# A two-layer float32 trunk on one core: seven products for the first mixer's values, paired half-height rate products, and router tiles moved by ScalarE

## The chip, the cores and the metric

One core of one Trainium2 chip runs the whole program, in float32. The metric is the device time of one execution in microseconds (us); of the kernel before, three runs stand here and their median counts. Lower is better. The engines are TensorE (PE in the rows, with its weight loads as PEld), VectorE (DVE), ScalarE (ACT), GpSimd (POOL) and SyncE (SP), which issues most DMAs. Each runs its own instructions strictly in order, and they wait for each other by semaphores.

## The reference

The input is 512 tokens of width 1024 and 256 memory tokens. There are two layers; layer 0 mixes tokens by RWKV-7, layer 1 by stick-breaking attention. Each mixer is followed by a cross-attention into the memory and by a mixture of experts (top 1 of 4 groups, then top 2 of 8 experts in it, 32 experts in all).

```python
def _rwkv7_time_mix(h, mix, wr, wk, wv, w0, w1, w2, a0, a1, a2, ...):
    xr, xw, xk, xv, xa, xg = [h + dx * mix[i] for i in range(N_MIX)]
    r = xr @ wr;  k = xk @ wk;  v = xv @ wv                  # 512x1024 by 1024x1024
    w_log = -softplus(-(w0 + tanh(xw @ w1) @ w2)) - 0.5      # rates: 64 inputs, 1024 outputs
    a = sigmoid(a0 + (xa @ a1) @ a2)                         # rates: 64 inputs, 1024 outputs
    kk = (k * k_k).reshape(B, S, H, N)
    kk = kk / maximum(norm(kk, axis=-1, keepdims=True), 1e-12)
    ...                                                      # state recurrence over heads
def _hierarchical_moe(h, wg, bg, we, be, w1, w3, w2):
    g_logits = t @ wg + bg;  e_logits = t @ we + be          # router: 4 + 32 columns
    ...                                                      # top-1 group, top-2 experts, SwiGLU
```

## The kernel before

The program has stages that follow each other on TensorE: the six projections of the first mixer, the "pair stage" (the recurrence for eight pairs of heads), the group norm, the memory's keys and values, the output product `rwo`, then for each layer cross-attention (`xq`, attention, `xo`), routing, and the experts.

**Large products.** A 1024x1024 weight arrives as two units of 2 MB in a ring of three. `project_T` (L568 to L573) takes eight output chunks of eight products each, 128x512 elements a product. Most other weights use Strassen-like "seven products": both operands are cut in quarters, VectorE forms eight sums of quarters (`sum_of`, L646, counted by the semaphore `quarters`), and TensorE takes 14 groups (`seven_T_pe`, L731 to L776: 8 products of 128x256 a group; `seven_pe`, L577: 4 products of 128x512 a group). Groups 4 to 7 wait for sum 5, groups 8 and 9 for sum 7, and groups 10 to 13 for sum 8. Eight of the groups are copied out by ScalarE (`T_out`, L779), the other six added onto them by VectorE (`add_T`, L786; `add_group`, L659). A group's bank is reused only when its last content has been copied or added.

**First mixer around the change.** TensorE's order is w1, a1, g1 (L891), wr and wk (seven products), then the rates (`rates_pe`, L935 and L936: for each of eight chunks one product with w2 and one with a2, both over 128 inputs, where half of each weight is zero), then two chunks of wv (L572), eight norm sums (`norms_pe`, L945), and six chunks of wv. ScalarE turns each chunk of rates into two sigmoids (L953, L955); TensorE's chunk j waits for the sigmoids of chunk j-2. Then ScalarE squares the keys (L959), copies two chunks of wv out, takes one square root over all norms (L912), makes the first pair's exponentials (L1052 to L1072), and copies out the rest of wv (L832). VectorE, after wk's last adds (L786): a scan and a difference (L1014, L1017) once all sigmoids are there, eight `max` operations on the norm sums (L970), then for each of eight chunks a reciprocal (L973) and a product (L975), and last five "factors" of pair 0 (L1024 to L1045), without which the pair stage (L1275) can't begin. TensorE's first pair product also waits for GpSimd's copy (L1110).

**Router around the change.** Group 8 to 13 of `xo` (L615) complete the rows of the hidden state h in order of tiles of 128 tokens: tile 0 is complete with group 8, tile 1 with 10, tile 2 with 11, tile 3 with 13 (`TILE_DONE`), each after VectorE's add (L659). Between these groups, at places that a table gives as (group, k), TensorE turns eight blocks of a tile (`late_turn`, L511), and later takes the router's logits of that tile (`route_logits`, L2025) and the ranks (`route_ranks`, L2042, L2043). Turned blocks lie in three banks, so block n waits until block n-3 has been moved out. Even blocks are moved by ScalarE (L521), odd ones by VectorE (L523); of tile 3 ScalarE moves all. VectorE runs the choice of experts as a chain of some 20 small operations a tile (`group_and_first`, L2133 to L2143, and `second`, L2148 to L2157), and `place` (L2162 to L2167). ScalarE squares and sums each tile (L2083, L2093), takes the root (L2087), scales the rows (L2073) and issues their store (L2075).

```python
    for n in range(4): mix(n, *MIXES[n])
    left_sums(vec, "wr", RK_S1)
    sums_T(vec, "wr", xm[1], RK_S1, RK_TS["wr"], R_)
    ...
    add_group(vec, xo, 8, 0, 1)
    evac(0)
    add_group(vec, xo, 9, 1, 1, 0, over=6)
    scale(0); group_and_first(0)
    add_group(vec, xo, 10, 1, 0, over=9)
    second(0)
    evac(1)
    add_group(vec, xo, 11, 2, 1)
```

## Time and profile before

| what | value |
|---|---|
| runs, us | 1753.58, 1757.02, 1759.72; median 1757.02 |
| profiled execution | 1754.93 us, span 1753.1 us |
| TensorE's granted clock, mean | 0.953 |
| busy share of the span: PE, DVE, ACT, POOL | 89%, 48%, 24%, 9% |
| chain that ended last: PE, issue, DVE, ACT | 70%, 7%, 5%, 4% |
| DMA | 312.89 MB, mean 178 GB/s |

A float32 product is two MATMUL instructions in the trace, so 64 products read as "x128". Timeline rows give start, time on the engine, engine, line, operation, operands and count; what stands in brackets is the idle time just before and what ended it. "PEclk" in the rows by stretch is TensorE's granted clock as a share of full speed: 1.00 is 2.4 GHz, 0.50 is 1.2 GHz.

### The profile page before, as it was taken

The page shows a single profiled execution, that of the slowest core. Times are in us where ns is not written, and L with a number is a line of the kernel's source. Part 1 is how long each engine was busy: PE and PEld are TensorE (multiplying, and loading weights), DVE is VectorE, ACT ScalarE, POOL GpSimd, SP SyncE. Part 2 cuts the span into 40 slices and gives each one's busy share as a digit, 9 for nine tenths or more (in the row PEclk, how much of TensorE's full clock was granted, in tenths as well). Part 3 has the DMA queues.
Part 4 walks back from the last instruction along what each step waited for, and adds up shares of the span by engine and source line. Part 5 has one row for each costly group of instructions (what it writes and reads, how often), then busy time and mean ns, then how long its engine had stood idle before and what let it go on. Part 6 is the DMA issues. An engine that isn't in the chain of part 4 may idle for free.

```text
span 1753.1 us, 28204 instructions
## 1 busy us (share of the span) xinstructions
PE 1568.8 (89%) x12141; PEld 953.5 (54%) x12141; DVE 833.0 (48%) x1416; ACT 421.3 (24%) x833; POOL 165.1 (9%) x185
## 2 busy tenths in 40 slices
PE   4999989998799999879877899999999996988785
PEld 2786468887474685444323368745558544333332
DVE  5651766664384625444222174447643554431225
ACT  2103245554300212211000130117421312100002
POOL 2000132330000000011111100000000001111101
PEclk8999999999799999969998999999999996999898
DMA  7026200000532521259999952220024124999994
GB/s 241 1 96 240 90 3 4 4 4 4 216 116 76 214 74 52 101 225 412 423 424 423 371 199 96 96 95 2 1 109 180 25 87 171 391 423 425 425 413 185
DMA packets 81503, 312.89 MB, mean 178 GB/s; under 512 B 17776, under 2 KB 18856, under 8 KB 56608
## 3 DMA queue, kind: packets, MB, share of 16 engines
q1 hardware_dynamic: 69280, 282.76, 41.1%
q0 software_dynamic: 10944, 24.10, 3.7%
q10 hardware_dynamic: 1152, 4.19, 0.6%
q8 instruction: 97, 1.59, 0.4%
q14 instruction: 30, 0.25, 0.0%
HBM read 305.81 MB, written 33.29 MB: 193 GB/s over the span
## 4 chain that ended last, share of the span: by engine, by line
PE 70%; issue 7%; DVE 5%; ACT 4%; DMA 1%; POOL 1%; PEld 0%; DVEq 0%; POOLq 0%; ACTq 0%
PE PS L2482 14%; PE PS L615 13%; PE PS L748 10%; PE PS L1275 7%; PE PS L2507 6%; PE PS L1609 2%; PE PS L572 2%; PE PS L2467 2%; PE PS L586 2%; PE PS L1585 1%; PE PS L1857 1%; PE PS L1878 1%; PE PS L511 1%; PE PS L1868 1%; PE PS L2025 1%
## 5 line engine op out<-in xcount | busy, mean ns | idle before, releaser
L748 PE MATMUL PS<-arena,ring 128*128 128x256 f32 x1152 | 251.2, 379 | 0.0
L748 PEld LDWEIGHTS PS<-arena,ring 128*128 128x128 f32 x1152 | 218.4, 190 | 31.2 <-issue 1.4
L615 PE MATMUL PS<-ring,arena 128*128 128x512 f32 x400 | 177.8, 596 | 0.7 <-ACT arena L1823 0.7
L2482 PE MATMUL PS<-ring,arena 128*64 128x512 f32 x512 | 127.8, 657 | 43.6 <-issue 40.5
L2482 PE MATMUL PS<-arena 128*64 128x512 f32 x512 | 125.7, 647 | 21.1 <-issue 18.3
L2490 DVE TENSOR_TENSOR arena<-PS,arena 128x256 f32<-128x256 f32 x32 | 13.6, 424 | 252.5 <-PE PS L2497 232.4
L615 PEld LDWEIGHTS PS<-ring,arena 128*128 128x128 f32 x400 | 75.5, 192 | 89.0 <-issue 88.0
L2482 PEld LDWEIGHTS PS<-ring,arena 128*64 128x64 f32 x512 | 43.0, 151 | 126.5 <-issue 122.8
L2487 ACT ACTIVATE arena<-PS 128x256 f32<-128x256 f32 x32 | 12.3, 384 | 359.1 <-PE PS L2482 359.1
L2482 PEld LDWEIGHTS PS<-arena 128*64 128x64 f32 x512 | 42.8, 148 | 102.4 <-issue 98.9
L572 PE MATMUL PS<-arena,ring 128*128 128x512 f32 (+1 forms) x256 | 84.5, 492 | 0.0
L786 DVE TENSOR_TENSOR arena<-arena,PS 128x512 f32<-128x512 f32 x48 | 31.5, 684 | 106.8 <-PE PS L748 106.8
L1275 PE MATMUL PS<-ring 64*64 64x64 f32 (+1 forms) x3072 | 75.4, 239 | 5.3 <-ACT ring L1124 3.1
L659 DVE TENSOR_TENSOR h<-h,PS 128x512 f32<-128x512 f32 x64 | 43.2, 685 | 76.9 <-PE PS L615 76.8
L779 ACT ACTIVATE arena<-PS 128x512 f32<-128x512 f32 x48 | 28.3, 596 | 211.8 <-PE PS L748 211.8
L1275 PEld LDWEIGHTS PS<-ring 64*64 64x64 f32 x3072 | 70.9, 137 | 13.6 <-issue 5.3
L1124 ACT ACTIVATE ring<-PS 128x512 f32<-128x512 f32 (+1 forms) x88 | 63.0, 753 | 50.8 <-PE PS L1275 48.4
L615 PE MATMUL PS<-arena 128*128 128x512 f32 x160 | 74.7, 612 | 0.0
L2382 POOL MEMSET arena<- 128x1024 f32 x4 | 3.8, 969 | 721.3 <-PE PS L615 721.3
L646 DVE TENSOR_TENSOR arena<-arena 128x1024 f32<-128x1024 f32 x40 | 49.0, 1224 | 47.6 <-PE PS L748 41.3
L572 PEld LDWEIGHTS PS<-arena,ring 128*128 128x128 f32 x256 | 49.7, 195 | 34.3 <-issue 30.6
L521 ACT ACTIVATE arena<-PS,gainT 128x128 f32<-128x128 f32 x88 | 27.7, 364 | 134.5 <-PE PS L511 134.3
(326 smaller groups left out, 2413.4 us busy)
## 6 DMA issues: line engine op xcount, KB each, us to landing
arena<-in_moe_w SPq DMA_DIRECT2D x96, 1024.0 KB, 16.2
ring<-in_moe_w SPq DMA_DIRECT2D x96, 1024.0 KB, 14.7
ring<-in_sb_wqkv SPq DMA_DIRECT2D x6, 2048.0 KB, 9.2
ring<-in_xa_wkv SPq DMA_DIRECT2D x4, 2048.0 KB, 15.6
ring<-in_xa_wq SPq DMA_DIRECT2D x4, 2048.0 KB, 8.7
ring<-in_xa_wo SPq DMA_DIRECT2D x4, 2048.0 KB, 14.5
h<-in_x SPq DMA_DIRECT2D x8, 512.0 KB, 5.0
ring<-in_rw_wr SPq DMA_DIRECT2D x2, 2048.0 KB, 14.4
```

What stands on the lines that cost most here:

```text
L572: ins = pe.matmul(PS[:, BANK_OF[g], 0:n], ring[:, u % RING, k, P * (j % 4):P * (j % 4) + P], xt[:, k, 0:n], start=(k == 0), stop=(k == KC ...
L586: ins = pe.matmul(PS[:, BANK_OF[g], :], xt[:, k, P * t:P * t + P], ring[:, (u0 + half) % RING, k, :], start=(k == 0), stop=(k == KC - 1))
L615: ins = pe.matmul(PS[:, BANK_OF[g], :], rows(k), cols[:, k, :], start=(k == 0 and not grows), stop=(k == 3), skip_group_check=grows)
L646: vec.tensor_tensor(out, a, b, op).then_inc(S("quarters"), 1)
L659: ins = vec.tensor_tensor(v, v, group_out(vec, g), ALU.add)
L748: ins = pe.matmul(PS[:, BANK_OF[g], M * c:M * c + M], rows[:, k, o:o + P], cols[:, k, :], start=(c + k == 0 and not grows), stop=(k == 3), ...
L1124: act.activation(dst, src, ACT.Copy).then_inc(S("pair_act_out"), 1)
L1275: return pe.matmul(out, lhs, rhs, start=start, stop=True, skip_group_check=True)
L1609: ins = pe.matmul(PS[:, BANK_OF[g], :], memV[:, m, XD * x + P * v:XD * x + P * v + P], probT[x % 2][:, m, :], start=(m == 0), stop=(m == 1))
L2467: ins = pe.transpose(bank(k // 4, 4, P)[:, k % 4, 0:rows], xg[p][0:rows, k::KC], ident[0:rows, 0:rows])
L2482: ins = pe.matmul(bank(2, 2, F)[r, :, :], xgT[p][:, k, r], w[a][:, :, k, :], start=(k == 0), stop=(k == KC - 1))
L2507: ins = pe.matmul(PS[r, 6 + half, :], hidT[:, k, r], w2e[p][a][:, k, 512 * half:512 * half + 512], start=(k == 0), stop=(k == 1))
```

## The change

It does three things. (1) wv gets 14 groups and eight sums like wr and wk; its sums and adds are put into VectorE's order around the norms, with the eighth sum and the last adds behind the loop of reciprocals. (2) The two rate products of a chunk take only the 64 inputs that are not zero, one on the lower and one on the upper half of the rows; GpSimd no longer clears the other halves. (3) In both routers tile 0 is still shared, but tiles 1 and 2 are moved by ScalarE alone, as tile 3 was; ScalarE squares a tile before it moves the blocks (tile 3 after); and TensorE turns a tile in four quarters of two blocks, one behind each k of a group. GpSimd's clearing of GT moves behind wv.

```diff
-    ("wr", 14, "AAVVAAAAAVVAVV"), ("wk", 14, "AAVVAAAAAVVAVV"), ("wv", 8, "A"),
+    ("wr", 14, "AAVVAAAAAVVAVV"), ("wk", 14, "AAVVAAAAAVVAVV"), ("wv", 14, "AAVVAAAAAVVAVV"),
...
-            pool.memset(w2s[HD:P, :], 0.0).then_inc(S("rates_padded"), 1)
-            pool.memset(a2s[0:HD, :], 0.0).then_inc(S("rates_padded"), 1)
...
+        def late_on_act(n):
+            return n % 2 == 0 or (LATE[n // (NT * KC)][:3] == "ffn" and n % (NT * KC) >= KC)
...
-        def late_turn(pe, name, t, ready):
+        def late_turn(pe, name, t, ready, ks=range(KC)):
             ready(pe, t)
-            for k in range(KC):
+            for k in ks:
...
+        WV_S1, WV_TS = at(28, [4, 512]), in_place(xm[1], at(30, [4, M]))
...
                     rates_pe(pe)
-                    project_T(pe, g, UNITS.index(name), x_, T, ready, range(2))
-                    norms_pe(pe)
-                    project_T(pe, g, UNITS.index(name), x_, T, ready, range(2, 8))
+                    seven_T_pe(pe, name, x_, WV_S1, WV_TS, ready, {(3, 1): lambda: norms_pe(pe)})
...
-            evac_T(act, FIRST["wv"], V_, chunks=range(2))
+            T_out(act, "wv", V_, range(2))
...
-            evac_T(act, FIRST["wv"], V_, chunks=range(2, 8))
+            T_out(act, "wv", V_, range(2, 8))
...
-                pe.matmul(PS[:, 4 + 2 * (j % 2), :], w2s[:, P * j:P * j + P], twa, start=True, stop=True)
-                pe.matmul(PS[:, 5 + 2 * (j % 2), :], a2s[:, P * j:P * j + P], twa, start=True, stop=True)\
+                pe.matmul(PS[:, 4 + 2 * (j % 2), :], w2s[half(0), P * j:P * j + P], twa[half(0), :], start=True, stop=True)
+                pe.matmul(PS[:, 5 + 2 * (j % 2), :], a2s[half(1), P * j:P * j + P], twa[half(1), :], start=True, stop=True)\
...
             vec.wait_ge(S("notfirst_ready"), 2)
+            left_sums(vec, "wv", WV_S1)
             vec.wait_ge(S("pre_sig"), 2 * KC)
             sums(vec, 0)
+            sums_T(vec, "wv", xm[1], WV_S1, WV_TS, V_)
             for j in range(KC):
                 vec.wait_ge(S("pre_summed"), j + 1)
                 vec.tensor_scalar(KK[:, j, :], PS[:, 4 + j % 4, :], 1e-24, None, ALU.max).then_inc(S("pre_norm"), 1)
...
                                          in1=KK[:, j, :], op0=ALU.mult, op1=ALU.mult).then_inc(S("kk_ready"), 1)
+            last_sum(vec, "wv", xm[1], WV_TS)
+            last_adds(vec, "wv", V_)
...
-            pool.wait_ge(S("proj_filled"), FIRST["wv"] + 8)
+            pool.wait_ge(S("proj_filled"), FIRST["wv"] + 14)
+            pool.memset(GT, 0.0).then_inc(S("zeros_ready"), 1)
...
-                     {(9, 1): lambda: late_turn(pe, ffn, 0, ready), (10, 1): lambda: route_logits(pe, l, 0),
-                      (11, 1): lambda: late_turn(pe, ffn, 1, ready), (12, 1): lambda: route_logits(pe, l, 1),
-                      (12, 2): lambda: late_turn(pe, ffn, 2, ready), (12, 3): lambda: route_ranks(pe, l, 0),
+                     {**turns(9, 0), **turns(11, 1), **turns(12, 2), (10, 1): lambda: route_logits(pe, l, 0),
...
                 ready(act, t)
-                late_evac(act, name, t, xTE, 0, 1 if last else 2)
+                if last:
+                    late_evac(act, name, t, xTE, 0, 1)
                 act.activation(tnE[:, t, 0:end], h[:, t, 0:end], ACT.Square, accum_out=total)
+                if not last:
+                    late_evac(act, name, t, xTE, 0, 1 if t else 2)
...
-            evac(1)
             add_group(vec, xo, 11, 2, 1)
             scale(1)
             group_and_first(1)
             second(1)
-            evac(2)
             place(0)
```

In `turns(12, 2)` the logits of tile 1 come behind the second quarter and the ranks of tile 0 behind the fourth.

The order of instructions shows where each piece lands. The first place is VectorE at the end of the first mixer's projections, in the changed kernel; L966 and L968 are the reciprocals and their products (L973 and L975 before), L638 is a sum of quarters, L779 an add of a group, L1019 to L1040 the five factors, L1188 the first operation of the pair stage.

```order
L966 RECIPROCAL arena<-arena 128x512
L968 SCALAR_TENSOR_TENSOR arena<-arena,prm 128x512
L638 TENSOR_TENSOR arena<-arena 128x1024
L779 TENSOR_TENSOR arena<-arena,PS 128x2x256 x6
L1019 TENSOR_TENSOR arena<-h 128x512
L1021 TENSOR_TENSOR arena<-h 128x512
L1026 SCALAR_TENSOR_TENSOR arena<-arena,prm,h 128x512
L1033 SCALAR_TENSOR_TENSOR arena<-arena,h 128x512
L1040 TENSOR_TENSOR arena<-arena,h 128x512
L1188 TENSOR_TENSOR ring<-PS,masks 128x8x64
```

Before, the factors came right behind the last reciprocal and product; now the eighth sum and six adds stand between.

The second place is TensorE in `xo`, groups 11 to 13 of layer 0, before the change: L615 are the products of `xo`, L511 the turns, L2025 the logits, L2042 and L2043 the ranks.

```order
L615 MATMUL PS<-ring,arena 128x512 x2
L511 MATMUL PS<-ident,h 128x128 x8
L615 MATMUL PS<-ring,arena 128x512 x4
L2025 MATMUL PS<-arena 128x36 x8
L615 MATMUL PS<-ring,arena 128x512
L511 MATMUL PS<-ident,h 128x128 x8
L615 MATMUL PS<-ring,arena 128x512
L2042 MATMUL PS<-arena,masks 128x32
L2043 MATMUL PS<-arena,ones 128x32
```

And the same place in the changed kernel, from group 12 on, with its own line numbers:

```order
L607 MATMUL PS<-ring,arena 128x512
L503 MATMUL PS<-ident,h 128x128 x2
L607 MATMUL PS<-ring,arena 128x512
L503 MATMUL PS<-ident,h 128x128 x2
L2029 MATMUL PS<-arena 128x36 x8
L607 MATMUL PS<-ring,arena 128x512
L503 MATMUL PS<-ident,h 128x128 x2
L607 MATMUL PS<-ring,arena 128x512
L503 MATMUL PS<-ident,h 128x128 x2
L2046 MATMUL PS<-arena,masks 128x32
L2047 MATMUL PS<-arena,ones 128x32
```

The turns of tile 2 have moved from one place to four, and two of its quarters now stand ahead of the logits of tile 1.

The third place is ScalarE in the same stretch in the changed kernel: L2088 squares a tile, L513 moves blocks, L2094 is the root, L2077 scales rows and L2079 stores them.

```order
L2088 ACTIVATE arena,sumsq<-h 128x1024
L513 ACTIVATE arena<-PS,gainT 128x128 x8
L2094 ACTIVATE rms<-sumsq,ffn_eps 128x1
L2077 ACTIVATE arena<-h,rstd 128x1024
L2079 DMA normed_rows<-arena 128x1024
L2088 ACTIVATE arena,sumsq<-h 128x1024
L513 ACTIVATE arena<-PS,gainT 128x128 x8
```

Tile 2's square, and behind it the moves of tile 2's blocks, come after the scaling and the store of tile 0's rows, as they did; but there are eight moves a tile now in place of four, and the square stands ahead of them.

## Rows read from the trace of the kernel before

**Rows 1.** The chain of waits: start, us, what.

```profile
199.89 27.44 issue
...
763.53 3.56 DMA arena<-normed_rows,table
```

**Rows 2.** Timeline of the first mixer's rates and of the values' first chunks.

```profile
151.59 1.02 PE L935 MATMUL PS<-arena 128*128 128x512 f32 x2
...
155.23 0.69 ACT L953 ACTIVATE arena<-PS,prm 128x512 f32<-128x512 f32 x1 [0.37 <-PE PS L936]
...
155.81 0.68 ACT L955 ACTIVATE arena<-PS,prm 128x512 f32<-128x512 f32 x1
...
165.32 13.90 PE L572 MATMUL PS<-arena,ring 128*128 128x512 f32 x32
...
166.90 1.22 DVE L1014 TENSOR_TENSOR_SCAN h<-h,arena 128x512 f32<-128x512 f32 x1 [13.67 <-ACT arena L955]
...
179.06 7.03 PE L945 MATMUL PS<-arena,hones 128*128 128x512 f32 x16
```

**Rows 3.** Timeline from the last norm to the first pair product.

```profile
185.93 41.36 PE L572 MATMUL PS<-arena,ring 128*128 128x512 f32 x96
...
186.85 3.62 ACT L912 ACTIVATE arena<-arena 128x4096 f32<-128x4096 f32 x1 [5.69 <-DVE arena L970]
...
190.50 3.35 DVE L973 RECIPROCAL arena<-arena 128x512 f32<-128x512 f32 x1 [3.68 <-ACT arena L912]
...
222.31 0.75 DVE L975 SCALAR_TENSOR_TENSOR arena<-arena,prm 128x512 f32<-128x512 f32 x1
...
225.44 0.68 DVE L1045 TENSOR_TENSOR arena<-arena,h 128x512 f32<-128x512 f32 x1
...
228.22 1.68 PE L1275 MATMUL PS<-arena 64*64 64x128 f32 x80 [0.94 <-POOL arena L1110]
```

**Rows 4.** Timeline, TensorE in wr and wk: products of 128x256.

```profile
82.53 41.60 PE L748 MATMUL PS<-arena,ring 128*128 128x256 f32 x192
```

**Rows 5.** Timeline, VectorE's sums for wk.

```profile
110.77 2.29 DVE L646 TENSOR_TENSOR ring<-arena,ring 128x2048 f32<-128x2048 f32 x1
113.09 2.48 DVE L646 TENSOR_TENSOR arena<-arena 128x1024 f32<-128x1024 f32 x2
```

**Rows 6.** By stretch: busy us of PE, PEld, DVE, ACT, POOL, then PEclk, DMA.

```profile
33.00:38.00 5.00, 4.71 (x6) 1.44 (x7) 5.00 (x9) 0.00 (x0) 0.00 (x0) 0.50 0.52 191
738.00:740.00 2.00, 2.00 (x6) 1.19 (x5) 0.69 (x3) 1.62 (x4) 0.00 (x0) 0.50 0.24 41
```

**Rows 7.** Timeline of layer 0's router up to the last tile.

```profile
722.13 0.69 DVE L659 TENSOR_TENSOR h<-h,PS 128x512 f32<-128x512 f32 x1
...
725.96 1.05 ACT L2083 ACTIVATE arena<-h 128x1024 f32<-128x1024 f32 x1
...
727.34 1.14 ACT L2073 ACTIVATE arena<-h,rstd 128x1024 f32<-128x1024 f32 x1
...
729.51 1.87 PE L2025 MATMUL PS<-arena 128*128 128x36 f32 x16
...
735.81 0.60 DVE L523 TENSOR_SCALAR arena<-PS,gainT 128x128 f32<-128x128 f32 x2
...
736.21 0.63 PE L511 MATMUL PS<-ident,h 128*128 128x128 f32 x3 [2.89 <-DVE arena L523]
...
739.24 0.22 DVE L2162 TENSOR_TENSOR arena<-arena,PS 128x64 f32<-128x64 f32 x1 [1.43 <-PE PS L2043]
...
743.94 0.26 DVE L2133 SCALAR_TENSOR_TENSOR arena<-PS,rstd,arena 128x36 f32<-128x36 f32 x1 [1.38 <-PE PS L2025]
...
747.46 0.60 PE L511 MATMUL PS<-ident,h 128*128 128x128 f32 x3 [1.46 <-DVE h L659]
```

**Rows 8.** Timeline of layer 1's router: end of tile 1's logits, turn of tile 3.

```profile
1443.42 1.10 PE L615 MATMUL PS<-ring,arena 128*128 128x512 f32 x2
...
1460.66 0.60 PE L511 MATMUL PS<-ident,h 128*128 128x128 f32 x3 [1.46 <-DVE h L659]
```

More of the change, by code:

```diff
@@ L775, in chunks, with T_out @@
             return dst[:, 2 * i:2 * i + 2, M * half:M * half + M]
-        def T_out(act, name, dst):
-            for n, i, half in ((0, 0, 0), (1, 1, 0), (4, 2, 0), (5, 3, 0), (6, 2, 1), (7, 3, 1), (8, 0, 1), (11, 1, 1)):
+        def T_out(act, name, dst, which=range(8)):
+            copied = (0, 0, 0), (1, 1, 0), (4, 2, 0), (5, 3, 0), (6, 2, 1), (7, 3, 1), (8, 0, 1), (11, 1, 1)
+            for n, i, half in copied[which.start:which.stop]:
                 act.activation(chunks(dst, i, half), group_out(act, FIRST[name] + n).rearrange("p (c n) -> p c n", c=2),
@@ L2176, in moe_choice_vec @@
             add_group(vec, xo, 8, 0, 1)
-            evac(0)
+            late_evac(vec, f"ffn{l}", 0, xTE, 1)
             add_group(vec, xo, 9, 1, 1, 0, over=6)
```

31 lines of the change are left out of this document (14 added, 17 removed).

## Prediction

> **What bounds the kernel now.** I read the page first: TensorE is busy 89% of the span, no other engine above half, and the chain of waits is TensorE's for 70%. So a change pays or costs only where it lets TensorE's sequence, or the engine TensorE waits for, run on sooner or later. Then I read the timeline of the two stages that the change touches. The chain's largest piece of 27.4 us in the first mixer is named "issue" [rows 1]: TensorE runs the values' chunks back to back, waiting for nothing. Beside it VectorE is hardly less loaded: from 190.50 to 222.98 it runs eight reciprocals with their products, 4.06 us each, and its last factor ends at 226.1, only 2.1 us ahead of the first pair product at 228.2 [rows 3]. The reader should see that VectorE has almost no slack there. In the router it is the reverse: TensorE waits, 2.9 us at 736.2 alone, for a block that VectorE moves late, behind its own chain of small operations [rows 7].
>
> **Part 1, the rates.** Sixteen products of 0.86 us (two instructions of 0.43) go from 151.59 to 165.32 [rows 2]. On two halves of the array they could overlap. The trace shows no products of 64 inputs by 128 outputs; the nearest row is 80 instructions on quarters of the array, 64 to 128 columns each, which end within 1.68 us [rows 3]; one by one they would need 6.0 us by their columns (32 of 128 and 48 of 64, at 0.43 us for 512), so the parts do run together. I take full overlap; nothing gained (0 us) is the other end. A chunk then takes 1.29 us from its first instruction to its last, but ScalarE needs 1.17 us for its two sigmoids (0.58 apart, [rows 2]) and chunk j waits for those of chunk j-2, so two chunks take 1.29 + 1.17 + two hand-overs of about 0.13, 2.7 us. The values' products start at 162.0 in place of 165.3, and the sigmoids end 3.3 us earlier too, at 163.5. The Trainium skill's page "TensorEngine Tiling (Array Packing)", under "Theoretical Speedup", gives up to twice the speed for 64 inputs, and under "PSUM Bottleneck" says that the emptying of PSUM may then become the limit. By the table alone the values would start at 158.5, and the sum below would be 3.5 us lower; by the second sentence, which the sigmoids' rows bear out, it stays.
>
> **Part 2, the values, up to the norms.** 64 products of 128x512 become 112 of 128x256. At 192 instructions in 41.6 us one takes 0.217 us [rows 4], so a group (16 instructions) takes 3.47 us and all 14 take 48.5, against 128 of 0.431 us, 55.1 [rows 3]: 6.6 us less work for TensorE. In return VectorE gets eight sums and ten adds. Two sums of 2.3 us [rows 5] fit into its idle 13.7 us before the scan [rows 2]: they cost nothing while that wait lasts and would cost 4.6 us without it. They need both units of the weights where the old chunks began with one; the second is asked for when wk's group 11 is done, ahead of everything else in SyncE's queue, and I take it to be there in time. Groups 0 to 3 take 13.9 us, as the two old chunks did, and end at 175.9. Behind the scan come sums of 1.2, 2.3, 1.2 and 1.2 us [rows 5] and two adds (0.7 us, as L1045 in [rows 3]), the second of which needs group 3, so it ends at 176.8, and sum 7 (2.3 us) at 179.0. Only then do the `max` operations begin. The fifth norm product needs the first of them, at 179.7, and four products of 0.86 us bring the last norm to 183.2, where it was 185.93 [rows 2, 3]: 2.7 us earlier.
>
> **Part 3, the eighth sum.** This decides. In the changed order, sum 8 stands behind the last reciprocal product, and groups 10 to 13 wait for it. From the last norm, VectorE and ScalarE need 4.6 us to the first reciprocal (one `max`, one root of 3.6 us), then 32.5 us for the reciprocals [rows 3], then 1.2 us for the sum: sum 8 is there at 221.5. TensorE has groups 4 to 9 to run meanwhile, 20.8 us plus about 2.5 us in which group 6 waits for ScalarE to leave the exponentials, and is done at 206.5. It idles for 15 us. Groups 10 to 13 take 13.9 us more. After such a gap the clock falls: when the work began at 33.3 after idle time, it was granted 0.50 until 38 [rows 6], which cost half of 4.8 us, so I add 2.4 (0 to 3). That is 237.8. Then comes what was hidden before: the last add (0.3 until it starts, 0.7) and the five factors, 3.1 us [rows 3], behind it in VectorE's order. The first pair product starts at 242.0 against 228.2: 13.8 us late. GpSimd's clearing and copy (about 1.6 us) fit beside the factors. A second gap of 4 us now stands ahead of the pair stage; after the 2.9 us gap at 736.2 the clock was 0.50 from 738 to 740 [rows 6, 7], so I add 1.5 us for small products at 1.2 GHz (0, if it holds, to 6, if the stage runs its first iteration so). First mixer: **+15.3 us** (+11 to +21). The removed clearing of two halves by GpSimd is worth nothing: TensorE's first work doesn't wait for it.
>
> The same tiling page says under "Key Properties" that a change of tiling mode drains TensorE. That would add a few tenths of a microsecond at each end of the rates, and no term of mine holds it.
>
> **Part 4, the routers.** For layer 0, TensorE's logits of tile 1 end at 731.2 (729.51 and sixteen instructions) and its turn of tile 3 begins at 747.46 [rows 7], 16.2 us later. Of these VectorE spends 4.6 us on the choice for tile 1 (to 735.8), then moves tile 2's blocks, for TensorE is stuck on them, and only at 739.24 places tile 0. From there to the turn it needs 8.2 us, of which it waits 1.4 us for logits [rows 7]. With the moves gone and the logits earlier, both waits go: 4.6 + 6.8 = 11.4 us from the logits of tile 1 to the turn of tile 3, 4.8 us less. Late next is ScalarE. Tile 1's turn can start at about 722.5 (add at 722.13 less a little). ScalarE then squares (1.05 and a read-out of 0.2, [rows 7]), moves eight blocks as TensorE turns them over group 11, takes the root at about 727.1, scales and stores tile 0's rows (from 727.34 it took 1.5 us, [rows 7]), and squares tile 2 to about 730.1. The first block of tile 2 is moved at 730.5, TensorE's third turn there waits for it some 2 us, and tile 1's logits, behind that quarter, end at 732.4, 1.1 us later than before. Net 3.6 us for layer 0. In layer 1 the same stretch is 17.2 us long (1443.42 to 1460.66, [rows 8]), 1.0 us more, so 4.6 us. What follows is kept: the gather of rows (763.53, [rows 1]) waits for the table, and the later weights' loads wait for the gather, so the whole experts' stage moves with it. Routers: **-8.2 us** (-3, if ScalarE is later still, to -13).
>
> **The sum.** +15.3 - 8.2 = +7.1 us on the profiled execution of 1754.9, which is 1762.0. The profiled execution lies 2.1 us under the median of the three runs, 1757.0; on the median the sum is 1764.1, and I give 1764.
>
> **The rivals.**
> *Forecast, 0.60:* TensorE idles some 15 us before group 10; slower by 5.3 us or more. 0.3%, 5.3 us, is about what a measurement of this kernel tells from no change.
> *The gap is there but cheap, 0.27:* the clock costs little (mixer +11.3, without the 2.4 and the 1.5) and the routers give their 8.2 or somewhat more. +3 to -1 us, 1756 to 1760: no change to be measured. For it: the clock stays at 1.00 through shorter waits. Against it: the granted 0.50 after the gap at 736.
> *The values no longer bound, 0.08, on the other side:* if groups 10 to 13 could follow group 9, TensorE would end the values at 183.2 + 34.7 = 217.9, the last add and the factors would end at 222, the mixer would gain 6.2 us, and with the routers the kernel would take 1742 to 1745. It decides by whether sum 8 is there before 204; the order speaks against it, for VectorE runs no instruction out of turn, and eight reciprocals of 3.35 us have no room to shrink. A weaker form is that the routers give 8 us or more each (every wait in 35 us gone, at most 9.5 each) against +11: 1749 to 1752.
> *No overlap of the halves, 0.05 as a case of its own, slower:* the rates take their 13.7 us, all of part 2 comes 3.3 us later, and with a cold start of the pair stage the time is 1770 to 1775.
> All cases together give faster 0.08, same 0.27, slower 0.65. The range reaches from the cheap gap to the cold pair stage, 1755 to 1773.
>
> **What would show it.** Right: in the changed trace a wait of TensorE before group 10 of wv of about 15 us, released by VectorE's sum (a 128x1024 TENSOR_TENSOR behind the last product of the reciprocals); a granted clock of 0.50 in the first 5 us after it; the first pair product near 242; rates at a step of 1.3 to 1.4 us; no wait of TensorE on VectorE's moves in the turns of tiles 1 and 2, and one of about 2 us on ScalarE's there; the turn of tile 3 some 4 us earlier against the start of `xo`. Wrong: a first pair product before 230, or a distance from the start of `xo` to the gather that hasn't shrunk.

## Result and profile after

The changed kernel took 1766.66 us (median of 7 runs, 1757.69 to 1774.28), the kernel before, run beside it, 1756.74 us: a ratio of 1.0051, 95% interval 1.003 to 1.0071. Timed again later in 12 runs it took 1763.96 us against 1756.90, a ratio of 1.0044 (1.0027 to 1.0062). So it is slower, by 8 or 9 us. The profiled execution is the fastest of its seven runs, 1757.69 us with a span of 1755.9; the span of the one before was 1753.1. So stretches of the traces are compared here, not their totals. The two profiles are also shifted against each other: the first rate product starts at 150.39 us in the changed kernel and at 151.59 in the one before. So distances from there are compared here, and not moments.

The page of the changed kernel, parts 1 and 5 (busy time, share of the span, instructions; then group, busy time and mean ns, idle time just before it and its releaser):

```profile
PE 1553.6 (88%) x12237; PEld 965.2 (55%) x12237; DVE 849.1 (48%) x1416; ACT 424.4 (24%) x849; POOL 162.7 (9%) x183
...
L740 PE MATMUL PS<-arena,ring 128*128 128x256 f32 x1344 | 295.5, 381 | 14.9 <-DVE arena L638 14.9
```

TensorE has less work than before and waits 14.9 us in one place: L740 are the products of quarters, L638 VectorE's sums. Before, the values' products waited for nothing [rows 1].

**The rates.** Timeline of the changed kernel, TensorE and ScalarE (start, time, engine, line, operation, count, idle time before), answering to [rows 2]. "64*128" is the part of the array used, 64 rows by 128 columns:

```profile
150.39 0.69 PE L926 MATMUL PS<-arena 64*128 64x512 f32 x1
...
150.93 0.59 PE L926 MATMUL PS<-arena 64*128 64x512 f32 x1
...
154.12 0.69 PE L926 MATMUL PS<-arena 64*128 64x512 f32 x1
154.15 0.69 ACT L944 ACTIVATE arena<-PS,prm 128x512 f32<-128x512 f32 x1
...
156.62 0.69 PE L926 MATMUL PS<-arena 64*128 64x512 f32 x1
...
160.17 14.08 PE L740 MATMUL PS<-arena,ring 128*128 128x256 f32 x64
```

L926 is the first product of a chunk; its partner on the other half stands in L927. The rates now take from 150.39 to 160.17, 9.8 us, where they took 13.7. Two chunks come every 2.50 us (154.12 to 156.62): TensorE's first product of the next pair of chunks waits until ScalarE has ended its sigmoids (L944, L946), which start every 0.58 us and fill 2.3 of the 2.50.

**The norms and the reciprocals.** The same timeline, VectorE, ScalarE and TensorE, answering to [rows 3]:

```profile
152.18 2.29 DVE L638 TENSOR_TENSOR arena<-ring 128x2048 f32<-128x2048 f32 x1 [0.24 <-DMA ring<-in_rw_wv]
...
178.00 3.67 PE L936 MATMUL PS<-arena,hones 128*128 128x512 f32 x8 [0.31 <-DVE arena L963]
...
186.08 3.35 DVE L966 RECIPROCAL arena<-arena 128x512 f32<-128x512 f32 x1 [3.68 <-ACT arena L904]
...
190.90 7.17 PE L740 MATMUL PS<-arena 128*128 128x256 f32 x32 [2.32 <-ACT arena L772]
...
217.89 0.75 DVE L968 SCALAR_TENSOR_TENSOR arena<-arena,prm 128x512 f32<-128x512 f32 x1
218.56 1.22 DVE L638 TENSOR_TENSOR arena<-arena 128x1024 f32<-128x1024 f32 x1
219.83 16.07 PE L740 MATMUL PS<-arena,ring 128*128 128x256 f32 x64 [14.86 <-DVE arena L638]
...
236.01 0.69 DVE L779 TENSOR_TENSOR arena<-arena,PS 128x512 f32<-128x512 f32 x1 [2.14 <-PE PS L740]
...
239.50 0.68 DVE L1040 TENSOR_TENSOR arena<-arena,h 128x512 f32<-128x512 f32 x1
240.32 2.44 PE L1270 MATMUL PS<-arena 64*64 64x128 f32 x80 [4.42 <-DVE arena L1040]
```

The reader should follow VectorE (DVE): the last reciprocal's product at 217.89, then the eighth sum at 218.56, and TensorE's group 10 starts when that sum ends, 14.86 us after group 9. Behind group 13 the last add and five factors are no longer hidden: TensorE waits another 4.42 us. From the first rate product to the first pair product are 89.9 us (240.32 less 150.39), where there were 76.6 (228.22 less 151.59).

The clock in the same stretch of the changed kernel (stretch, its length, then busy time and count of PE, PEld, DVE, ACT and POOL, granted clock, DMA share, GB/s):

```profile
210.00:220.00 10.00, 0.17 (x1) 0.17 (x2) 9.93 (x7) 0.00 (x0) 0.00 (x0) 0.51 0.00 0
...
220.00:222.00 2.00, 2.00 (x5) 1.64 (x6) 0.97 (x2) 0.00 (x0) 0.00 (x0) 0.50 0.00 0
222.00:224.00 2.00, 2.00 (x6) 1.55 (x6) 0.00 (x0) 0.00 (x0) 0.00 (x0) 0.53 0.00 0
224.00:226.00 2.00, 2.00 (x11) 1.77 (x10) 0.35 (x1) 0.00 (x0) 0.00 (x0) 1.00 0.00 0
...
240.00:242.00 2.00, 1.68 (x64) 1.71 (x68) 0.18 (x1) 0.00 (x0) 0.00 (x0) 0.74 0.00 0
242.00:244.00 2.00, 1.37 (x40) 1.18 (x37) 1.94 (x4) 0.00 (x0) 0.00 (x0) 0.50 0.03 8
```

TensorE comes back from the long wait at half speed and is at full speed again from about 224. Groups 10 to 13 take 16.07 us, 2.0 more than the 14.08 of groups 0 to 3, which are as many instructions at full speed.

**The router of layer 0**, the changed kernel's timeline, TensorE and ScalarE, answering to [rows 7] (L503 turns, L2029 logits, L607 products of `xo`; L2077 scales rows, L2088 squares, L513 moves blocks):

```profile
736.19 1.14 ACT L2077 ACTIVATE arena<-h,rstd 128x1024 f32<-128x1024 f32 x1
...
737.34 0.27 PE L503 MATMUL PS<-ident,h 128*128 128x128 f32 x1
...
737.76 1.06 ACT L2088 ACTIVATE arena<-h 128x1024 f32<-128x1024 f32 x1 [0.43 <-ACT arena L2077]
...
738.81 1.18 ACT L513 ACTIVATE arena<-PS,gainT 128x128 f32<-128x128 f32 x4
...
739.21 0.38 PE L503 MATMUL PS<-ident,h 128*128 128x128 f32 x1 [1.60 <-ACT arena L513]
739.43 1.87 PE L2029 MATMUL PS<-arena 128*128 128x36 f32 x16
...
752.82 2.66 PE L503 MATMUL PS<-ident,h 128*128 128x128 f32 x8 [2.68 <-DVE h L651]
```

VectorE's 2.89 us wait is gone. A wait of 1.60 us for ScalarE has come: the fourth block of tile 2 needs a bank that ScalarE empties only after it has scaled tile 0's rows and squared tile 2, and tile 1's logits stand behind that block. The router still comes out ahead: from the start of `xo` to the gather of layer 0 it is 689.1 to 768.99 us, 79.9, where it was 679.7 to 763.53, 83.8; in layer 1 80.7 where it was 84.7. By the traces, then, the first mixer loses 13.3 us and the routers give back 3.9 and 4.0, +5.4 in all. That lies at the lower end of what was measured: the two intervals of the ratio are +5.3 to +12.5 and +4.7 to +10.9 us.

### The profile page after: what moved, and what is told of

The parts are those of the page before. It is cut to its first block, busy times and chain, and to the rows that moved or that the text cites. A ratio compares the mean times of both kernels' runs of the same rounds, so it can differ in the third digit from the quotient of the medians.

```text
span 1755.9 us, 28430 instructions
## 1 busy us (share of the span) xinstructions
PE 1553.6 (88%) x12237; PEld 965.2 (55%) x12237; DVE 849.1 (48%) x1416; ACT 424.4 (24%) x849; POOL 162.7 (9%) x183
## 4 chain that ended last, share of the span: by engine, by line
PE 81%; DVE 7%; issue 6%; ACT 4%; DMA 1%; SPq 1%; PEld 0%; DVEq 0%; ACTq 0%; POOLq 0%
PE PS L740 18%; PE PS L2484 14%; PE PS L607 12%; PE PS L1270 7%; PE PS L2509 7%; PE PS L1605 2%; PE PS L2469 2%; PE PS L2433 2%; PE PS L564 2%; PE PS L578 2%; DVE arena L966 1%; PE PS L1581 1%; PE PS L1861 1%; PE PS L885 1%; PE PS L1882 1%
## 5 line engine op out<-in xcount | busy, mean ns | idle before, releaser
L740 PE MATMUL PS<-arena,ring 128*128 128x256 f32 x1344 | 295.5, 381 | 14.9 <-DVE arena L638 14.9
L740 PEld LDWEIGHTS PS<-arena,ring 128*128 128x128 f32 x1344 | 256.1, 191 | 53.1 <-DVE arena L638 15.7
L2484 PE MATMUL PS<-ring,arena 128*64 128x512 f32 x512 | 133.6, 681 | 54.1 <-issue 51.0
L607 PE MATMUL PS<-ring,arena 128*128 128x512 f32 x400 | 180.5, 598 | 0.7 <-ACT arena L1827 0.7
L2484 PE MATMUL PS<-arena 128*64 128x512 f32 x512 | 117.2, 611 | 14.3 <-issue 11.6
L607 PEld LDWEIGHTS PS<-ring,arena 128*128 128x128 f32 x400 | 74.8, 193 | 83.3 <-issue 82.3
L779 DVE TENSOR_TENSOR arena<-arena,PS 128x512 f32<-128x512 f32 x56 | 36.8, 684 | 121.3 <-PE PS L740 121.3
L772 ACT ACTIVATE arena<-PS 128x512 f32<-128x512 f32 x56 | 32.9, 595 | 248.1 <-PE PS L740 248.1
L638 DVE TENSOR_TENSOR arena<-arena 128x1024 f32<-128x1024 f32 x44 | 54.9, 1249 | 47.7 <-PE PS L740 41.3
L607 PE MATMUL PS<-arena 128*128 128x512 f32 x160 | 72.3, 595 | 0.0
L2509 PE MATMUL PS<-ring,arena 128*64 128x512 f32 x256 | 58.5, 598 | 1.0 <-issue 1.0
L1851 DVE TENSOR_TENSOR_SCAN arena<-arena 128x128 f32<-128x128 f32 (+3 forms) x64 | 48.3, 809 | 22.9 <-ACT arena L1813 22.9
L2509 PE MATMUL PS<-arena 128*64 128x512 f32 x256 | 58.5, 598 | 1.0 <-issue 1.0
## 6 DMA issues: line engine op xcount, KB each, us to landing
ring<-in_xa_wo SPq DMA_DIRECT2D x4, 2048.0 KB, 13.8
ring<-in_rw_wr SPq DMA_DIRECT2D x2, 2048.0 KB, 13.3
```

What stands on the lines that cost most here:

```text
L607: ins = pe.matmul(PS[:, BANK_OF[g], :], rows(k), cols[:, k, :], start=(k == 0 and not grows), stop=(k == 3), skip_group_check=grows)
L638: vec.tensor_tensor(out, a, b, op).then_inc(S("quarters"), 1)
L740: ins = pe.matmul(PS[:, BANK_OF[g], M * c:M * c + M], rows[:, k, o:o + P], cols[:, k, :], start=(c + k == 0 and not grows), stop=(k == 3), ...
L779: ins = vec.tensor_tensor(v, v, group_out(vec, FIRST[name] + n).rearrange("p (c n) -> p c n", c=2), ALU.add)
L1851: vec.tensor_tensor_scan(att[m][a][:, 0:nn][:, ::-1], fail[m][a][:, T - nn:T][:, ::-1], from_query[:, T - nn:T][:, ::-1], 1.0, ALU.mult, A ...
L2484: ins = pe.matmul(bank(2, 2, F)[r, :, :], xgT[p][:, k, r], w[a][:, :, k, :], start=(k == 0), stop=(k == KC - 1))
```

## Experiments

Each was timed in five rounds beside the kernel before, whose median lay between 1754.8 and 1757.0 us. Ratios are to that kernel; 0.001 is 1.76 us, and the 95% intervals reach 0.002 to 0.003 to either side.

### Each part alone

**Rates alone** (kernel before with this):

```diff
-                pe.matmul(PS[:, 4 + 2 * (j % 2), :], w2s[:, P * j:P * j + P], twa, start=True, stop=True)
+                pe.matmul(PS[:, 4 + 2 * (j % 2), :], w2s[half(0), P * j:P * j + P], twa[half(0), :], start=True, stop=True)
...
-            pool.memset(w2s[HD:P, :], 0.0).then_inc(S("rates_padded"), 1)
```

> The kernel before with the rate products alone on 64 inputs, one on each half of the rows. My theory: in the changed kernel the eight chunks took 9.8 us from the first rate product to the first product of the values, against 13.7 before, because the halves overlap and ScalarE's two sigmoids a chunk set the step (1.25 us). Everything behind moves with it, VectorE's reciprocals too, so the first pair product comes 3.9 us sooner after the first rate product (72.7 us in place of 76.6) and the time is about 4 us lower, 0.2%. Rival: VectorE and ScalarE set the end of the values' stage in any case, so nothing is left of it at the first pair product (76.6 us).

Measured 1753.22 us against 1756.21, ratio 0.9986 (0.9965 to 1.0006). The sign isn't settled by the times. The trace of this kernel settles the mechanism: rates from 152.55 to 162.33, first pair product at 225.33, so 72.8 us between the first rate product and the first pair product, where the kernel before needs 76.6. The 3.9 us that the rates' stage is shorter (9.8 for 13.7) arrive at the first pair product but for 0.1, since the values' chunks hide nothing in front of them.

**Routers alone** (the changed kernel's `late_on_act`, quarter turns, order on ScalarE and VectorE, in the kernel before):

```diff
-                      (11, 1): lambda: late_turn(pe, ffn, 1, ready), (12, 1): lambda: route_logits(pe, l, 1),
...
+                     {**turns(9, 0), **turns(11, 1), **turns(12, 2), (10, 1): lambda: route_logits(pe, l, 0),
...
-            evac(1)
...
-            evac(2)
```

> The kernel before with the two routers' part alone. Theory: the whole is a sum of independent stages, and this one gives 3.9 us in layer 0 and 4.0 us in layer 1 (the shortening from the start of xo to the gather that the changed kernel's trace shows), so about 8 us less, 0.45%. Rival: part of what the routers gave in the changed kernel's trace was luck of the clock, and it gives under 4 us in all.

Measured 1747.76 us, ratio 0.9949 (0.9928 to 0.9969): about 9 us gained.

**Values alone** (the changed kernel's PLAN, sums and adds for wv, the rates on the whole array):

```diff
-    ("wv", 8, "A"),
+    ("wv", 14, "AAVVAAAAAVVAVV"),
...
+            last_sum(vec, "wv", xm[1], WV_TS)
+            last_adds(vec, "wv", V_)
```

> The kernel before with the values' seven products alone (rates and routers as before). Theory: the distance from the first rate product to the first pair product grows from 76.6 to about 94 us (89.9 in the changed kernel, plus the 3.9 that the rates gave there), so the time is 14 to 17 us higher, 0.8 to 1.0%. Rival: the rates' gain is swallowed in the changed kernel by the wait for the eighth sum, so without it the distance is no longer than there, 90 us, and the time 10 to 13 us higher.

Measured 1777.24 us, ratio 1.0117 (1.0088 to 1.0146): about 20.5 us lost. From the timeline of this kernel, TensorE:

```profile
223.76 15.78 PE L748 MATMUL PS<-arena,ring 128*128 128x256 f32 x64 [14.86 <-DVE arena L646]
243.96 2.69 PE L1279 MATMUL PS<-arena 64*64 64x128 f32 x80 [4.42 <-DVE arena L1049]
```

The wait is 14.86 us here too. From the first rate product (150.5) to the first pair product are 93.5 us, 16.9 more than before, as expected; the median lost some 4 us beyond that, but the interval, 15.5 to 25.6 us, takes the 16.9 in. By the ratios the parts add up to -2.5 - 9.0 + 20.5 = +9.0 us, and the whole change measured +9.0 and +7.7. Each part is known to 4 or 5 us only, so that the sum hits so well is partly luck; that the loss is in the values and the routers make back a good part of it is clear.

### The eighth sum among the reciprocals

The changed kernel, with work only reordered on VectorE:

```diff
                                          in1=KK[:, j, :], op0=ALU.mult, op1=ALU.mult).then_inc(S("kk_ready"), 1)
+                if j == 3:
+                    last_sum(vec, "wv", xm[1], WV_TS)
+                if j == 4:
+                    group_evacuated(vec, FIRST["wv"] + 4)
+                    add_T(vec, "wv", 9, V_, 2, 1, 0, over=6)
+                if j == 6:
+                    add_T(vec, "wv", 10, V_, 2, 0, over=9)
-            last_sum(vec, "wv", xm[1], WV_TS)
-            last_adds(vec, "wv", V_)
+            group_evacuated(vec, FIRST["wv"] + 5)
+            add_T(vec, "wv", 12, V_, 3, 1, 0, over=7)
+            add_T(vec, "wv", 13, V_, 3, 0, over=12)
```

> The changed kernel with the eighth sum of the values moved between the fourth and the fifth reciprocal, the add of group 9 behind the fifth and that of group 10 behind the seventh; nothing is taken away. Theory: the loss is TensorE's 14.9 us wait for that sum. It then has the sum at 203.5, before it ends group 9, groups 10 to 13 follow without a gap and at full clock and end near 218.5, and VectorE's reciprocals, adds and factors end near 227: first pair product 76 to 77 us after the first rate product in place of 89.9, time 12 to 15 us under the changed kernel, 4 to 8 us under the kernel before. Rival: VectorE's total work sets the end (sums, adds and reciprocals, whatever their order), so the first pair product moves by 3 us at most, and the time stays above that of the kernel before.

Measured 1751.5 us (12 runs, 1742.39 to 1756.87), ratio 0.9959 (0.9939 to 0.9978), some 15 us under the changed kernel. Timeline of this kernel, VectorE and TensorE:

```profile
203.48 1.22 DVE L638 TENSOR_TENSOR arena<-arena 128x1024 f32<-128x1024 f32 x1
...
221.94 0.75 DVE L968 SCALAR_TENSOR_TENSOR arena<-arena,prm 128x512 f32<-128x512 f32 x1
222.61 2.00 DVE L779 TENSOR_TENSOR arena<-arena,PS 128x512 f32<-128x512 f32 x3
...
199.02 17.43 PE L740 MATMUL PS<-arena,ring 128*128 128x256 f32 x80
218.69 3.72 PE L740 MATMUL PS<-arena,ring 128*128 128x256 f32 x16 [2.24 <-DVE arena L779]
227.82 2.90 PE L1278 MATMUL PS<-arena 64*64 64x128 f32 x80 [5.41 <-DVE arena L1048]
```

Group 10 now follows group 9 without a wait (80 instructions in one row), and the distance from the first rate to the first pair product falls from 89.9 to 76.3 us. With the same work in another order the wait and the loss both go, so the 14.86 us wait is shown to be the cause. The last three rows show something more: TensorE is done with the values at 222.4 and waits 5.41 us for VectorE. The seven products save TensorE work that VectorE, busy without a break from 187.2 to 227.7, doesn't let it use: the distance is 76.3 us though the overlapped rates, which took 3.85 us off it by themselves, are in it.

### Is the idle time dear because of the clock?

Two kernels fill TensorE's idle time with products whose results nothing reads. In the changed kernel:

```diff
+            if name == "wv":
+                pe.wait_ge(S("pre_norm"), KC)
+                for n in range(15):
+                    pe.matmul(PS[:, 4, :], hones[:, :], left(name, 0, 0)[:, n % 4, :], start=True, stop=True)
             summed_quarters(pe, name, after[2])
             group(10, 0, left(name, 1, 1), t4)
...
+            for n in range(14):
+                pe.matmul(PS[:, 4, 0:P], hones[:, :], hones[:, :], start=True, stop=True)
             pe.wait_ge(S("zeros_ready"), 3)
```

> The changed kernel with work added and none removed: 15 products of 128x512 that nothing reads fill TensorE's idle 14.86 us between group 9 and group 10 of the values (15 x 0.90 us = 13.5), and 14 small ones (14 x 0.22 = 3.1 us) the 4.42 us before the first pair product. The wait for the eighth sum stays. Theory (the idle gaps cost more than their length, because TensorE comes back from them at 1.2 GHz, and in some runs the pair stage starts at that clock): groups 10 to 13 take 13.9 us instead of 16.07, the window from 220 on stays at a granted clock of 1.00, the first pair product comes about 2 us earlier than 240.3, near 238; the median falls from 1766.7 to 1757 to 1761, and the runs, which lay over 17 us, lie closer together. Rival (the clock of later stages has nothing to do with these gaps): only the 2 us, so 1764 to 1765, with the runs as far apart as before. If the added products were themselves in the way (their bank, the heat), the time would rise over 1767.

Measured 1763.35 us (12 runs, 1757.82 to 1767.93), ratio 1.0027 (1.0009 to 1.0046). Timeline of this kernel, TensorE:

```profile
207.76 13.04 PE L763 MATMUL PS<-ring,hones 128*128 128x512 f32 x30
222.79 15.77 PE L740 MATMUL PS<-arena,ring 128*128 128x256 f32 x64 [1.99 <-DVE arena L638]
239.46 3.36 PE L1289 MATMUL PS<-hones 128*128 128x128 f32 x28 [0.90 <-issue]
242.98 1.68 PE L1274 MATMUL PS<-arena 64*64 64x128 f32 x80 [0.17 <-DVE arena L1044]
```

The theory isn't borne out, and it isn't refuted either, for the clock was not kept up. The gap is filled but for 1.99 us, yet groups 10 to 13 take 15.77 us, not 13.9 or 14.1, at a granted clock of 0.84 and 0.87 in the two windows from 220 to 232, and from the first rate product to the first pair product it takes 89.6 us, 0.3 less than in the changed kernel; both the theory and the rival had expected 2. The median is 0.6 and 3.3 us under the two measurements of the changed kernel, the ratio 3 and 4 us under theirs, with intervals that overlap. The lowest runs of the two kernels are alike (1757.8, and 1756.7 and 1757.7); only the tail above 1768 us is missing. Before the pair stage the clock was kept up: 80 products take 1.68 us where they took 2.44. Yet the stage takes 220.9 us, where the two profiles of the changed kernel have 219.8 and 221.9. So no cost of the gaps beyond their length and the 2.0 us of groups 10 to 13 can be seen.

The second fills only the 5.4 us ahead of the pair stage, in the kernel with the moved sum:

```diff
+            for n in range(17):
+                pe.matmul(PS[:, 4, 0:P], hones[:, :], hones[:, :], start=True, stop=True)
             pe.wait_ge(S("zeros_ready"), 3)
```

> The changed kernel with its eighth sum and two adds among the reciprocals (the experiment that took 1751.5, with runs in two groups at 1742.4 to 1743.0 and 1748 to 1757), and with 17 products of 128x128 that nothing reads on TensorE in the 5.41 us before the first pair product (17 x 0.22 = 3.7 us). In the profile of that experiment the granted clock was 0.50 from 226 to about 238 us. Theory (the slow group of runs is a pair stage entered at 1.2 GHz after that gap): with the gap filled all runs fall in the fast group, median 1742 to 1745, spread under 6 us. Rival (the two groups have another cause, later in the program): they stay, and the median is 1749 to 1753.

Measured 1752.16 us (12 runs, 1747.68 to 1759.35), ratio 0.9981 (0.9964 to 0.9998): no gain, and the runs do not gather near 1743. The 17 products began after 2.3 us more of idle time and took 5.66 us in place of 3.7, so the first pair product came at 230.30, 2.5 us late. In its profile the pair stage (to the first sum of the group norm) then took 222.6 us against 228.4. That doesn't show what an entry at full speed is worth: two kernels that both enter it so took 219.7 and 228.9 us (last section).

### The routers, piece by piece

First the routers' part with whole turns at the old places, everything else as in the routers alone:

```diff
-                     {**turns(9, 0), **turns(11, 1), **turns(12, 2), (10, 1): lambda: route_logits(pe, l, 0),
+                     {(9, 1): lambda: late_turn(pe, ffn, 0, ready), (10, 1): lambda: route_logits(pe, l, 0),
+                      (11, 1): lambda: late_turn(pe, ffn, 1, ready), (12, 1): lambda: route_logits(pe, l, 1),
+                      (12, 2): lambda: late_turn(pe, ffn, 2, ready), (12, 3): lambda: route_ranks(pe, l, 0),
```

> The kernel before with the routers' part in which ScalarE alone moves tiles 1 and 2 and squares first, but TensorE turns each tile whole, eight blocks in a row at the old places, not in quarters among a group's products. With three banks and 0.31 us for a move by ScalarE a whole turn takes 2.66 us (the last tile's row of the changed kernel) instead of 1.8 us for four quarters that wait for nothing, and tile 1 and 2 wait besides for the squaring of 1.2 us ahead of their first move. Theory (the quarters carry the gain, the engine that moves the blocks only takes the 2.89 us wait for VectorE away): two thirds of the routers' 9 us are lost, 1752 to 1755, and the trace shows waits for ScalarE in the turns of tile 1 and 2. Rival (it is VectorE's release that matters, the quarters nothing): 1747 to 1749, like the routers' part as a whole.

Measured 1744.45 us (6 runs, 1739.28 to 1748.45), ratio 0.9935 (0.9913 to 0.9958). I had expected two thirds of the gain to go; none goes, and the stage is shorter still. Timeline of this kernel, TensorE in layer 0 (L506 turns, L2030 logits):

```profile
718.64 0.54 PE L506 MATMUL PS<-ident,h 128*128 128x128 f32 x3
720.02 1.47 PE L506 MATMUL PS<-ident,h 128*128 128x128 f32 x5 [0.83 <-ACT arena L516]
...
724.76 1.87 PE L2030 MATMUL PS<-arena 128*128 128x36 f32 x16
...
728.13 1.47 PE L506 MATMUL PS<-ident,h 128*128 128x128 f32 x5 [0.24 <-ACT arena L516]
```

ScalarE alone keeps pace with a whole turn but for 0.83 and 0.24 us. From the first product of `xo` to the logits of tile 3 are 65.8 us, against 71.3 before and 68.4 with quarters. So the gain doesn't need the quarters; it comes with taking the moves off VectorE (squaring a tile first was not tried apart from that), and these quarters take some of it back.

Then the quarters, with one swap (the expectation names tile 1 for the rows that ScalarE scales before it squares tile 2; by the kernel's order they are tile 0's):

```diff
                 def quarter_turn(k):
+                    if (n, k) == (12, 1):
+                        route_logits(pe, l, 1)
                     late_turn(pe, ffn, t, ready, (2 * k, 2 * k + 1))
-                    if (n, k) == (12, 1):
-                        route_logits(pe, l, 1)
```

> The kernel before with the routers' part as the change has it, but in group 12 the logits of tile 1 are ahead of the second quarter of tile 2's turns, not behind it. In the trace of the routers' part alone the fourth block of tile 2 waits 1.60 us for ScalarE, which scales tile 1, issues its rows and squares tile 2 before it moves the first block, and the logits of tile 1 stand behind that; TensorE comes back at 1.2 GHz (2.69 us for logits that take 1.87). Theory (what the quarters lose to the whole turns is this one wait and the clock behind it): the logits' 1.87 us cover the wait, no idle time is left there, from the first output product to the logits of tile 3 it takes 65.5 to 66.5 us instead of 68.35 in layer 0, and the median is 1743 to 1746 like that of the whole turns (1744.45). Rival (two-block pieces among a group's products cost by themselves): the stage stays at 67.5 to 68.5 and the median at 1747 to 1748.

Measured 1741.89 us (6 runs, 1737.11 to 1745.04), ratio 0.9916 (0.9894 to 0.9938). Timelines of the routers alone, and behind it of this kernel, TensorE (L2028 logits, L610 products of `xo`):

```profile
728.09 0.38 PE L506 MATMUL PS<-ident,h 128*128 128x128 f32 x1 [1.60 <-ACT arena L516]
728.30 2.69 PE L2028 MATMUL PS<-arena 128*128 128x36 f32 x16
730.79 2.05 PE L610 MATMUL PS<-ring,arena 128*128 128x512 f32 x2
```

```profile
734.01 1.87 PE L2028 MATMUL PS<-arena 128*128 128x36 f32 x16
735.72 0.55 PE L506 MATMUL PS<-ident,h 128*128 128x128 f32 x2
736.11 1.02 PE L610 MATMUL PS<-ring,arena 128*128 128x512 f32 x2
```

With the logits first there is no wait, and the same logits take 1.87 us instead of 2.69, the same two instructions of `xo` 1.02 instead of 2.05. The granted clock behind the wait was 0.50 (730 to 734) in the routers alone; here it is 1.00 from 730 to 744. From the first product of `xo` to the logits of tile 3 are now 65.3 us in layer 0 for 68.4, so the wait of 1.60 us had cost 3.0, and quarters aren't dear by themselves. In layer 1 the swap took 1.5 us off; there the logits behind the wait had taken 1.87 and the two instructions of `xo` 1.64. That is 4.5 us by the traces and about 6 by the medians and the ratios, whose intervals overlap a little.

### Versions that keep only what pays

**Rates and routers on the kernel before**, as the change has them:

```diff
-                pe.matmul(PS[:, 4 + 2 * (j % 2), :], w2s[:, P * j:P * j + P], twa, start=True, stop=True)
+                pe.matmul(PS[:, 4 + 2 * (j % 2), :], w2s[half(0), P * j:P * j + P], twa[half(0), :], start=True, stop=True)
...
+                     {**turns(9, 0), **turns(11, 1), **turns(12, 2), (10, 1): lambda: route_logits(pe, l, 0),
```

> The kernel before with the rates' and the routers' part, without the values' seven products. The parts were measured apart as -2.4 us (rates) and -9 us (routers). If they add up: 0.993 of the kernel before, some 1745 us, and the trace shows the first norm product 24 us behind the first rate product and the gather of layer 0 near 757. If the router's gain hides the rates' one or the other way: 1747 to 1749. The values' part costs 20 us of which the seven products' removal is the whole, so this kernel should beat the changed one by some 21 us and the one before by some 11.

Measured 1748.13 us (9 runs, 1735.40 to 1757.77), ratio 0.9943 (0.9917 to 0.9969). Its first pair product, from its timeline:

```profile
223.98 1.68 PE L1266 MATMUL PS<-arena 64*64 64x128 f32 x80 [0.94 <-POOL arena L1101]
```

It comes 72.8 us after the first rate product, 3.5 us sooner than with the values' seven products and the moved sum (76.3). The old values are the better ones even then. The time itself is that of the routers alone (0.9949), as the second case of the expectation had it: the rates' 3.9 us are in the trace, but too small for these medians.

**Rates and whole turns:** the kernel before with the rates' edit and the whole turns of the experiment above.

> The kernel before with the rates' part and with the routers' part in its better form: ScalarE alone moves tiles 1 and 2 and squares first, TensorE turns each tile whole. Measured apart: rates -3 us, whole turns 1744.45 against 1757.0 (-12.5). If they add up 1741 to 1743, a ratio of 0.991 to 0.992 to the kernel before, and the first pair product near 224, the gather of layer 0 near 752. If the clock's changes from run to run swallow the rates' part, 1744 to 1745, no better than the whole turns alone.

Measured 1740.98 us (6 runs, 1734.74 to 1748.37), ratio 0.9922 (0.9892 to 0.9951). It beats both kernels: 16 us under the one before by the medians, 14 by the ratio, and 23 to 26 under the changed one. The first pair product came at 224.6, as expected; the gather of layer 0 came at 757.0 and not near 752, for the pair stage took 225.4 us in its profile, 5.7 more than in the one of whole turns. The quarters with the logits first, without the rates (1741.89), can't be told from it.

**The whole change with both waits mended** (the moved sum and the swapped logits):

> The whole change with both of its waits mended: the eighth sum and two adds of the values among the reciprocals (1751.5 by itself), and the logits of tile 1 ahead of the second quarter of tile 2 (1741.9 against 1747.8 without that, -5.9, in the routers' part alone). If the two are independent: 1745 to 1747, a ratio of 0.993 to 0.994 to the kernel before, so better than both kernels, but 4 to 6 us behind the kernel with rates and routers and the values as before (1740.98). Rival (the seven products of quarters are worth their 8 saved groups once nothing waits for the router): 1740 or less, level with it.

Measured 1744.80 us (10 runs, 1734.35 to 1752.42), ratio 0.9947 (0.9923 to 0.9971). This lies where two independent gains put it, but its interval overlaps that of the kernel with rates and whole turns. That the values' seven products are worth less than nothing with the sum moved is shown by the traces (3.5 us) and not by the times.

## Why the prediction was right, point by point

It forecast +7.1 us and a first place of loss, and both were found: +9.0 and +7.7 by ratio. The mechanism is shown by the experiments. That the number came so near is in part luck: the traces give +5.4, and the 1.5 us put on top for the pair stage stand for something that no run shows.

- **Part 1, the rates.** The halves overlap in full: two instructions side by side come every 0.43 us, where one did before, and two chunks take 2.50 us where I had 2.7. The term that was too large is the 1.29 us for a chunk. It equals three steps of 0.43, as if its four instructions still came one behind the other; from a chunk's first instruction to its first sigmoid it took 1.18 (155.46 to 156.64). The stage gained 3.9 us instead of 3.3; ScalarE's sigmoids set the pace, as reasoned. The drain at a change of mode, which the prediction names and puts into no term, shows as a small delay: at the change to halves the next two steps are 0.31 and 0.53 us where 0.22 and 0.43 are usual, at the change back 0.52 and 0.32 where 0.43 and 0.22 are. That is 0.2 us at each end.
- **Part 2.** The two early sums cost nothing, and the second unit of weights was just there (VectorE waited 0.24 us for it). Counted from the first rate product, the values went on behind the last norm after 31.1 us (at 181.51), where I had 31.6 and the kernel before 34.3. VectorE's first `max` came after 26.8, where I had 27.4.
- **Part 3.** The eighth sum was done 69.4 us after the first rate product (forecast 69.9), the idle time was 14.86 us (15), the granted clock 0.50 and 0.53 in the first 4 us behind it (0.50 for 5), groups 10 to 13 took 16.07 (16.3), and from the first rate product to the first pair product it took 89.9 us against 76.6, +13.3 for +13.8. The eighth sum moved took it away. The 1.5 us for a slow entry into the pair stage could not be confirmed: the granted clock was 0.74 and 0.50 in its first 4 us, but the stage as a whole took 219.8 us in this profile and 221.9 in the second one of the same kernel, where the kernel before took 222.6, and other profiles of it vary by more. No run shows this term.
- **Part 4.** -3.9 us in layer 0 and -4.0 in layer 1, for -3.6 and -4.6. The distance on which the sum was built, from the end of tile 1's logits to the turn of tile 3, is 11.7 us in layer 0, for the 11.4 of the sum. The wait for ScalarE was where it was expected, 1.60 us for "some 2". What I missed is what it can set off: in the profile after, the clock stayed at 1.00 behind it in layer 0 and was 0.50 for some 7 us in layer 1, and with the wait cured the routers gain 3.0 and 1.5 us more in their traces. I also took the quarters for a help; whole turns do better than these, and quarters with the swap do as well.
- **The rivals.** The cheap gap came near: it gave the mixer +11.3 and took off the two terms of the clock. Of these the 2.4 us came to 2.0 and the 1.5 could not be shown; with the routers' 7.9 that is +5.4, between this rival's +3 and the forecast's +7.1. The case in which values no longer bound fell with the 14.86 us. Its price was wrong too: the moved sum makes groups 10 to 13 follow group 9, and then VectorE's factors end at 227.7 and not at 222, so the mixer gains 0.3 us and not 6.2; for the sum and the six adds that VectorE now has between its first reciprocal and the factors take 4.9 us, which this rival had at nothing. No overlap fell with the rates' 9.8 us.

## What to carry to other kernels

Fewer products on TensorE pay only if the engine that prepares and adds their pieces has room; here eight reciprocals of 3.35 us held VectorE, and 6.6 us of saved products became a wait of 14.86 us and a second one of 4.42. Put a small operation that another engine waits for in the middle of a long loop, not behind it, and look at what stands behind each wait on the in-order engine: moving one block of logits ahead of a turn was worth 4.5 us in the traces, more than the overlapped rates gave. Measure the parts of a mixed change apart, since two gains of 11 us together hid half of a loss of 20.

## What the hardware showed

- Two instructions of 64 rows, one on each half of the array, start within 0.01 us of each other and the next two 0.43 us later, as single instructions of 128 rows do. Around each change between the whole array and halves the steps are 0.2 us longer in all.
- Runs of one kernel differ by up to 22 us (rates and routers), by 17 in the seven of the changed kernel, and the mean granted clock falls as the time rises. In those seven 0.954 went with 1757.7 us and 0.941 with 1774.3, some 1.3 us for each thousandth; the experiments' runs have slopes of 0.9 to 2. The pair stage shows a part of it: its instructions are the same in all kernels, and it took from 219.7 to 228.9 us in their profiles. In the slowest, that of the swapped logits, the windows read

```profile
233.00:236.00 3.00, 3.00 (x71) 2.88 (x73) 1.26 (x2) 2.00 (x4) 1.92 (x2) 0.50 0.00 0
236.00:239.00 3.00, 2.14 (x50) 1.72 (x46) 0.69 (x1) 1.36 (x3) 2.36 (x2) 0.50 0.01 3
```

  and with whole turns, from nearly the same start and the same work before it, 

```profile
233.00:236.00 3.00, 2.16 (x100) 1.88 (x100) 1.86 (x3) 2.67 (x5) 2.44 (x2) 1.00 0.00 0
236.00:239.00 3.00, 2.00 (x72) 1.82 (x72) 0.56 (x1) 1.67 (x4) 1.80 (x2) 1.00 0.03 8
```

  Nothing in the program differs there; which of the two a run gets was not found. It stays open. So the total of one profile proves nothing to within a few us here; a wait in its rows does.
- A wait of 1.60 us was followed by a clock of 1.00 in layer 0 of the changed kernel's profile, and the same wait, 1.58 us, by 0.50 in layer 1. So what a short wait costs behind its own length differs within one execution.
- With 13 of 15 us of the gap filled, the windows behind it were still granted 0.84 and 0.87. A remainder of 1.99 us was idle, and whether that alone lowered the clock was not tried.
